# Two pads of 32 bytes that shift every SBUF tile of a two-block transformer kernel

## The chip, the cores and the metric

The kernel runs on one core of one Trainium2 chip, as one program with one launch. Its metric is the device time in microseconds (us).

## The reference, cut to what matters

Two blocks work on 512 tokens of width 1024, in float32, one after the other. The first block has two layers and carries 256 context tokens through its first layer as well, so its matrices have 768 columns there and 512 in the second layer. Each layer is a modulated norm, a projection `px = h @ w_in + b_in`, three mixers (a bidirectional chunked mLSTM, a gated spatial unit, an axial convolution), an output projection and a feed-forward part:

```
x = x + g1 * (y_x @ w_out[l])
x = x + g2 * swiglu(rmsnorm(x) * (1 + sc2) + sh2, w_gu[l], w_down[l])    # 1024 -> 2 x 2816 -> 1024
```

The second block has a dilated windowed attention in three groups (`a_w_in` of 80 x 128 columns), then a sliding-window attention with sinks, and after each a layer norm and a gate:

```
x = layer_norm(ALPHA * x + mixer(x)); x = x + sigmoid(x @ ple_w_gate[i]) * (p[i] @ ple_w_proj[i])
```

Nearly all arithmetic is in these dense products.

## The kernel before, in words

Every activation lies feature-major: 128 features on the partitions, eight such tiles of 1024 features, tokens along the free axis. A dense product is cut into output tiles of 128 features. The weights of one such tile, eight blocks of 128 x 128, come by one DMA into one of four buffers `raw0` to `raw3` (SP's queue, `load`).

Float32 accuracy is made out of three one-pass products in the type `fp32r`. GpSimd (POOL) splits the weights in `split_weights`: `w_hi` is the rounded upper part (line 442), `w_lo = raw - w_hi` the rest (line 444), and `w_lo` is written over `raw`. It does so in two halves for each output tile, one tile ahead of TensorE. For some tiles of the second block ScalarE makes the upper part and POOL only the rest (`split_lower`, line 457). The activations are split too: `XH` and `XL` (normed input of a product), `HH` and `HL` (the feed-forward part's inner values), `XH2`/`XL2` and `YH2`/`YL2` (second block; `YH` and `YL` in the trace). `gemm_step` then issues, for each of the eight blocks, hi x H (line 463), hi x L (464) and lo x H (466), with 512 moving columns, and again with 256 where the context tokens are carried. The in-projection of the first block does the same in `three` (lines 1668 to 1670). A small product in the second block has its own weights `PWH`, `PWL` and operands `PH`, `PL` (lines 837 to 839). In every one of these the weights are the stationary operand and are loaded anew for each matmul.

Each engine runs its own list of instructions, and semaphores tie them together: POOL waits for TensorE to be done with the tile before last (`s_tile`), TensorE waits for the split (`s_split`) and for a free pair of PSUM banks (`s_evac`), ScalarE (ACT) empties the banks, VectorE (DVE) does residuals, norms and the lower halves. Nothing in these lists depends on an address.

All SBUF tiles are laid out by `place` (lines 208 to 217). A tile without `addr` goes to the cursor, which then moves on by the tile's size rounded up to 32 bytes; a tile with `addr` overlays another. The cursor starts at the first multiple of 64 past what the compiler holds back, which is byte 16512, or 129 x 128:

```
        raw = [place(f"raw{i}", [P, KT * P]) for i in range(RING)]
        w_hi = [place(f"w_hi{i}", [P, KT, P], FP32R) for i in range(2)]
        w_lo = [place(f"w_lo{i}", [P, KT, P], FP32R, addr=addr_of[f"raw{i}"]) for i in range(RING)]
        ...
        XH = place("XH", [P, KT, T], FP32R)
        XL = place("XL", [P, KT, T], FP32R)
```

Past `XL` come the small tiles and then, from `work` (line 271), the mixers' tiles, over which `HH` and `HL` lie. The second block starts its own layout at the address of `tri` (line 509) for `YH2`, `YL2`, `PWH`, `PWL`, `PH` and `PL`, and lays `X2`, `XH2` and `XL2` over `XH` and `XL`. Following the sizes gives the bytes past a multiple of 128 at which each operand starts; inside an operand every block is a multiple of 512 bytes further on, so a block's start has the same remainder.

| operand | address before | past a multiple of 128 |
|---|---|---|
| raw, w_lo, w_hi | 16512 to 36992 | 0 |
| Z, X | 41088, 57600 | 0 |
| ones | 57024 | 64 |
| XH, XL; XH2, XL2 | 82176, 106752; 98560, 114944 | 0 |
| HH, HL | 149184, 173760 | 64 |
| YH2, YL2 | 143808, 160192 | 64 |
| PWH, PWL; PH, PL | 198080, 189888; 208320, 212416 | 64 |
| YC, AC | 210720, 216864 | 32 |

Of the kernel before, what the change touches and what calls it, by code (L numbers as in the profile page):

```python
# [20 lines left out]
P = 128  # L21
# [181 lines left out]
def build_program(nc, xT, cT, cb_d, pc_d, fin_d, srow_d, consts_d, sguw_d, wg_d, wmod_d, win_d, wout_d, wgu_d, wdn_d,  # L203
# [4 lines left out]
    def place(name, shape, dt=FP32, addr=None):  # L208
        size = 4
        for s in shape[1:]:  # L210
            size *= s
        if addr is None:
            addr = cursor[0]
            cursor[0] += size + (-size) % 32
        assert addr + size <= nc.sbuf_usable_end, (name, addr + size, nc.sbuf_usable_end)
        addr_of[name] = addr
        return nc.alloc_sbuf_tensor_at(name, shape, dt, offset=addr)

    stack = ExitStack()
    with stack:  # L220
        def sem(name):
            return stack.enter_context(nc.semaphore(name))


        raw = [place(f"raw{i}", [P, KT * P]) for i in range(RING)]
        w_hi = [place(f"w_hi{i}", [P, KT, P], FP32R) for i in range(2)]
        w_lo = [place(f"w_lo{i}", [P, KT, P], FP32R, addr=addr_of[f"raw{i}"]) for i in range(RING)]
# [7 lines left out]
        XH = place("XH", [P, KT, T], FP32R)  # L235
        XL = place("XL", [P, KT, T], FP32R)

        tri = place("tri", [P, 2, P])
        mskd = place("mskd", [P, 2, P])
        mskr = place("mskr", [P, 2, P], FP32R, addr=addr_of["mskd"])  # L240
# [2786 lines left out]
```

## Time and profile before

| | |
|---|---|
| three runs | 2586.6 us median (2584.41 to 2588.71) |
| profiled execution, first to last instruction | 2586.4 us |
| TensorE (PE) busy | 2522.5 us, 98% of the span, 14594 matmuls |
| PE weight loads (PEld) busy | 2083.7 us, 81% |
| POOL busy | 1544.1 us, 60% |
| DVE busy | 1386.4 us, 54% |
| ACT busy | 776.3 us, 30% |
| DMA | 99 GB/s on average |

The profile is of one execution; its span lies 0.2 us from the median of the runs. Matmuls overlap in the pipeline, so the duration shown for one (some 400 ns) is longer than the distance between the starts of two that follow each other; that distance is called the pitch here, and it is read from the starts in the timeline. Busy shares are averages over stages.

### The profile page before, as it was taken

What the parts mean: (1) busy time and instruction counts of PE and PEld (TensorE: products, weight loads), DVE (VectorE), ACT (ScalarE), POOL (GpSimd) and SP (SyncE); (2) the same over time, 40 slices, a digit from 0 to 9 for tenths busy, and PEclk for the clock granted to TensorE, in tenths of its full rate; (3) what the DMA queues carried; (4) which work ended last, traced back from release to release, by engine and by line L of the source; (5) the groups of instructions that cost most, each with busy time, mean ns of one, the idle gap of its engine ahead of it and who ended that gap; (6) DMA issues with size and microseconds to landing.
All of it is one profiled execution on the core that took longest, in us unless ns stands there. A gap on an engine that the chain in (4) does not pass through costs nothing.

```text
span 2586.4 us, 39643 instructions
## 1 busy us (share of the span) xinstructions
PE 2522.5 (98%) x14594; PEld 2083.7 (81%) x14594; DVE 1386.4 (54%) x2065; ACT 776.3 (30%) x1620; POOL 1544.1 (60%) x1625
## 2 busy tenths in 40 slices
PE   6999999999999999999999999999999999999999
PEld 4888988888888886888788887778888888777876
DVE  5864556742853758726433333444444545556754
ACT  3224353111111123244321212222222222443544
POOL 3433245765766665543777777776666676556563
PEclk9999999999999999999999999999999999999999
DMA  7341142332333322121233232433333333323231
GB/s 280 107 155 41 34 179 86 127 130 65 122 130 98 119 60 69 58 66 42 83 96 94 93 98 82 130 106 100 91 103 96 93 103 94 98 73 98 83 106 65
DMA packets 79264, 255.57 MB, mean 99 GB/s; under 512 B 9872, under 2 KB 13712, under 8 KB 78864
## 3 DMA queue, kind: packets, MB, share of 16 engines
q1 hardware_dynamic: 63136, 213.21, 25.8%
q10 hardware_dynamic: 15984, 40.40, 5.1%
q8 instruction: 94, 1.54, 0.3%
q14 instruction: 50, 0.41, 0.1%
HBM read 236.28 MB, written 2.10 MB: 92 GB/s over the span
## 4 chain that ended last, share of the span: by engine, by line
PE 88%; DVE 4%; issue 3%; POOL 2%; ACT 2%; DMA 1%; SPq 0%; ACTq 0%; POOLq 0%; DVEq 0%
PE PS L463 21%; PE PS L466 21%; PE PS L464 21%; PE PS L1668 4%; PE PS L1670 4%; PE PS L1669 4%; PE PS L725 1%; POOL w_lo L444 1%; PE PS L714 1%; PE PS L708 1%; DMA raw<-in_wout 1%; PE PS L1524 1%; POOL w_hi L442 1%; DVE Z L2425 1%; DVE XL L2432 1%
## 5 line engine op out<-in xcount | busy, mean ns | idle before, releaser
L444 POOL TENSOR_TENSOR w_lo<-raw,w_hi 128x512 fp32r<-128x512 f32 (+1 forms) x606 | 880.5, 1453 | 50.6
L463 PE MATMUL PS<-XH,w_hi 128*128 128x512 f32 (+1 forms) x2080 | 782.7, 376 | 16.5 <-DVE XL L2432 3.3
L464 PE MATMUL PS<-XL,w_hi 128*128 128x512 f32 (+1 forms) x2080 | 755.6, 372 | 0.0
L466 PE MATMUL PS<-XH,w_lo 128*128 128x512 f32 (+1 forms) x2080 | 707.2, 373 | 0.0
L437 POOL TENSOR_TENSOR word<-ones 128x1 f32<-128x1 f32 x303 | 93.7, 309 | 869.4 <-PE PS L466 544.2
L463 PEld LDWEIGHTS PS<-XH,w_hi 128*128 128x128 f32 x2080 | 392.2, 189 | 118.6 <-issue 9.3
L442 POOL TENSOR_SCALAR w_hi<-raw 128x512 fp32r<-128x512 f32 (+1 forms) x606 | 482.0, 795 | 0.0
L464 PEld LDWEIGHTS PS<-XL,w_hi 128*128 128x128 f32 x2080 | 392.4, 189 | 70.0
L466 PEld LDWEIGHTS PS<-XH,w_lo 128*128 128x128 f32 x2080 | 362.5, 188 | 55.1
L1668 PE MATMUL PS<-XH,w_hi 128*128 128x512 f32 (+1 forms) x640 | 230.9, 361 | 8.4 <-DVE XL L2432 8.4
L1670 PE MATMUL PS<-XH,w_lo 128*128 128x512 f32 (+1 forms) x640 | 224.9, 351 | 0.0
L1669 PE MATMUL PS<-XL,w_hi 128*128 128x512 f32 (+1 forms) x640 | 224.8, 351 | 0.0
L2530 DVE TENSOR_TENSOR X<-X,Z 128x768 f32 (+3 forms) x60 | 86.0, 1433 | 228.6 <-ACT Z L2051 216.9
L463 PE MATMUL PS<-HH,w_hi 128*128 128x512 f32 (+1 forms) x528 | 187.6, 355 | 3.6 <-DVE HL L2896 3.6
L464 PE MATMUL PS<-HL,w_hi 128*128 128x512 f32 (+1 forms) x528 | 179.4, 354 | 0.0
L2494 DVE CUSTOM_DVE_ANT_0 cprod<-modv,cb 128x1024 f32<-128x1024 f32 x96 | 164.2, 1710 | 18.0 <-DMA modv<-in_wmod 15.1
L2891 DVE SCALAR_TENSOR_TENSOR Z<-TH,Z 128x768 f32<-128x768 f32 (+1 forms) x44 | 50.0, 1136 | 207.5 <-ACT Z L2032 206.4
L466 PE MATMUL PS<-HH,w_lo 128*128 128x512 f32 (+1 forms) x528 | 158.8, 355 | 0.0
L457 POOL TENSOR_TENSOR w_lo<-raw,w_hi 128x512 fp32r<-128x512 f32 x56 | 83.6, 1512 | 106.3 <-ACT w_hi L1051 84.9
L951 ACT ACTIVATE Z<-PS 128x512 f32<-128x512 f32 x99 | 58.7, 594 | 292.3 <-PE PS L466 279.5
L1668 PEld LDWEIGHTS PS<-XH,w_hi 128*128 128x128 f32 x640 | 121.5, 190 | 27.5 <-issue 9.6
L1670 PEld LDWEIGHTS PS<-XH,w_lo 128*128 128x128 f32 x640 | 121.3, 190 | 17.3
(346 smaller groups left out, 3507.0 us busy)
## 6 DMA issues: line engine op xcount, KB each, us to landing
raw<-in_wgu SPq DMA_DIRECT2D x88, 512.0 KB, 3.5
raw<-in_wa SPq DMA_DIRECT2D x80, 512.0 KB, 3.5
modt<-in_wmod SPq DMA_DIRECT2D x48, 512.0 KB, 9.9
raw<-in_win SPq DMA_DIRECT2D x48, 512.0 KB, 3.5
modv<-in_wmod ACTq DMA_DIRECT2D x48, 512.0 KB, 4.7
raw<-in_wdn SPq DMA_DIRECT2D x32, 512.0 KB, 3.6
QS<-Z ACTq DMA_DIRECT2D x96, 128.0 KB, 2.6
raw<-in_wout SPq DMA_DIRECT2D x16, 512.0 KB, 3.5
```

The costliest lines, as they stand in the source:

```text
L437: pool.tensor_tensor(word[:, 0:1], ones[:, 0:1], ones[:, 0:1], ALU.mult)
L442: pool.tensor_scalar(hi, src, 1.0, 0.0, ALU.mult, ALU.add).then_inc(s_hi, 1)
L444: pool.tensor_tensor(lo, src, hi.bitcast(FP32), ALU.subtract).then_inc(s_split, 1)
L457: pool.tensor_tensor(w_lo[s % RING][:, ks, :], src, w_hi[s % 2][:, ks, :].bitcast(FP32), ALU.subtract).then_inc(s_split, 1)
L463: pe.matmul(acc(s)[:, a:b], hi, rh[:, i, a:b], start=i == 0, stop=False)
L464: pe.matmul(acc(s)[:, a:b], hi, rl[:, i, a:b], start=False, stop=False)
L466: last = pe.matmul(acc(s)[:, a:b], lo, rh[:, i, a:b], start=False, stop=i == k - 1)
L1668: pe.matmul(out, hi, XH[:, i, a:b], start=first, stop=False)
L1669: pe.matmul(out, hi, XL[:, i, a:b], start=False, stop=False)
L1670: return pe.matmul(out, lo, XH[:, i, a:b], start=False, stop=i == KT - 1)
L2494: last = dve.tensor_tensor_reduce(out=cprod[:], in0=modv[slots + u][:], in1=cb[:, n, :], scale=0.5, scalar=0.0, op0=ALU.mult, op1=ALU.add, ...
L2530: dve.tensor_tensor(x, x, Z[:, s % 4, 0:w], ALU.add).then_inc(s_used, 1)
```

## The change

Two tiles of eight floats, 32 bytes, that nobody uses are placed: `lead` ahead of `raw0` and `lead2` ahead of `tri`. No instruction is added, removed or moved.

```diff
+        place("lead", [P, 8])
         raw = [place(f"raw{i}", [P, KT * P]) for i in range(RING)]
...
         XL = place("XL", [P, KT, T], FP32R)
 
+        place("lead2", [P, 8])
         tri = place("tri", [P, 2, P])
```

All from `raw0` to `XL` moves up by 32 bytes, all from `tri` on by 64. The weights, Z, X, XH, XL, XH2 and XL2 then start 32 bytes past a multiple of 128, HH, HL, YH2, YL2, PWH, PWL, PH and PL at a multiple of 128, YC and AC at 96 past one. The distance from the weights to XH and XL stays what it was; that to HH, HL, YH2 and YL2 grows by 32.

## Rows read from the trace of the kernel before

**Rows 1.** The page's head and engines, and its row of TensorE's granted clock
```profile
span 2586.4 us, 39643 instructions
PE 2522.5 (98%) x14594; PEld 2083.7 (81%) x14594; DVE 1386.4 (54%) x2065; ACT 776.3 (30%) x1620; POOL 1544.1 (60%) x1625
...
PEclk9999999999999999999999999999999999999999
```

**Rows 2.** The chain that ended last, by engine, and one of its pieces
```profile
PE 88%; DVE 4%; issue 3%; POOL 2%; ACT 2%; DMA 1%; SPq 0%; ACTq 0%; POOLq 0%; DVEq 0%
...
10.85 13.55 DMA modt<-in_wmod
```

**Rows 3.** PE's groups by form: names, shapes, count | busy us, mean ns | idle
```profile
L463 PE MATMUL PS<-XH,w_hi 128*128 128x512 f32 x1664 | 665.3, 400 | 16.5 <-DVE XL L2432 3.3 <-ACT TH L2353 2.6 <-DVE XL L1310 2.2
...
L1668 PE MATMUL PS<-XH,w_hi 128*128 128x512 f32 x384 | 156.8, 408 | 8.4 <-DVE XL L2432 8.4
...
L463 PE MATMUL PS<-HH,w_hi 128*128 128x512 f32 x352 | 138.0, 392 | 3.6 <-DVE HL L2896 3.6
...
L463 PE MATMUL PS<-XH,w_hi 128*128 128x256 f32 x416 | 117.4, 282 | 0.0
...
L463 PE MATMUL PS<-YH,w_hi 128*128 128x512 f32 x216 | 86.8, 402 | 0.8 <-POOL w_lo L457 0.8
...
L1668 PE MATMUL PS<-XH,w_hi 128*128 128x256 f32 x256 | 74.2, 290 | 0.0
...
L463 PE MATMUL PS<-HH,w_hi 128*128 128x256 f32 x176 | 49.7, 282 | 0.0
```

**Rows 4.** PE's timeline: start us, length us; first and last of 384 matmuls on XH, XL
```profile
1403.04 0.39 PE L463 MATMUL PS<-XH,w_hi 128*128 128x512 f32 x1
...
1492.03 0.40 PE L466 MATMUL PS<-XH,w_lo 128*128 128x512 f32 x1
```

**Rows 5.** PE's timeline: first and last of 162 matmuls on HH, HL
```profile
1500.22 0.39 PE L463 MATMUL PS<-HH,w_hi 128*128 128x512 f32 x1
...
1537.08 0.39 PE L466 MATMUL PS<-HH,w_lo 128*128 128x512 f32 x1
```

**Rows 6.** PE's timeline, 768 tokens: where HH, then XH, then HH again begins
```profile
551.76 0.40 PE L463 MATMUL PS<-HH,w_hi 128*128 128x512 f32 x1
...
618.34 0.39 PE L463 MATMUL PS<-XH,w_hi 128*128 128x512 f32 x1
...
752.61 0.39 PE L463 MATMUL PS<-HH,w_hi 128*128 128x512 f32 x1
```

**Rows 7.** PE's timeline: first and last of twelve matmuls on PH, PL
```profile
2253.45 0.39 PE L837 MATMUL PS<-PH,PWH 128*128 128x512 f32 x1
...
2255.94 0.39 PE L839 MATMUL PS<-PH,PWL 128*128 128x512 f32 x1
```

**Rows 8.** PE's groups by form: plain float32 matmuls against `ones`
```profile
L849 PE MATMUL PS<-Z,ones 128*128 128x512 f32 x32 | 14.3, 599 | 1.4 <-ACT Z L1091 1.4
...
L1663 PE MATMUL PS<-AC,ones 128*128 128x512 f32 x8 | 3.9, 592 | 0.0
```

**Rows 9.** Groups by form of DVE and ACT: tiles 32 past and others
```profile
L2731 DVE TENSOR_TENSOR AC<-AC,MU 128x512 f32<-128x512 f32 x2 | 1.3, 688 | 23.9 <-ACT MU L2201 23.9
L2891 DVE SCALAR_TENSOR_TENSOR Z<-TH,Z 128x512 f32<-128x512 f32 x22 | 15.3, 693 | 143.4 <-ACT Z L2032 143.4
...
L2278 ACT ACTIVATE YC<-AC 128x1024 f32<-128x1024 f32 x1 | 1.1, 1062 | 0.0
L2057 ACT ACTIVATE SQ<-X 128x512 f32<-128x512 f32 x14 | 8.9, 632 | 11.4 <-DVE X L2530 11.4
```

**Rows 10.** Groups of POOL, with its idle time and what ended it
```profile
L444 POOL TENSOR_TENSOR w_lo<-raw,w_hi 128x512 fp32r<-128x512 f32 (+1 forms) x606 | 880.5, 1453 | 50.6
L442 POOL TENSOR_SCALAR w_hi<-raw 128x512 fp32r<-128x512 f32 (+1 forms) x606 | 482.0, 795 | 0.0
L437 POOL TENSOR_TENSOR word<-ones 128x1 f32<-128x1 f32 x303 | 93.7, 309 | 869.4 <-PE PS L466 544.2 <-PE PS L1670 300.4 <-DMA raw<-in_win 16.3
```

**Rows 11.** Busy us and count by engine (PE, PEld, DVE, ACT, POOL), clock, DMA share, GB/s
```profile
1404.00:1491.00 87.00, 87.00 (x376) 70.54 (x375) 28.59 (x22) 17.41 (x31) 68.39 (x79) 1.00 0.31 97
```

## The prediction

> **What bounds the kernel now.** I read the engines' shares first, then the chain, then PE's groups and starts. PE is busy in 2522.5 of 2586.4 us, at its higher clock level of 2.4 GHz (granted 0.9 or more in every slice) [rows 1], and 88% of the chain is PE [rows 2]. In a stretch of dense product all 87.00 us of 87.00 are PE, POOL needs 68.39 of them, DVE 28.59, ACT 17.41 [rows 11]. So within the products the end is set by the pitch of the matmuls, and a nanosecond there is a nanosecond of the kernel, as often as there are matmuls. Counting each hi x H row three times (hi x L and lo x H have the same counts), there are on XH and XL (1664 + 384) x 3 = 6144 matmuls of 512 columns and (416 + 256) x 3 = 2016 of 256; on HH, HL, YH2, YL2 (352 + 216) x 3 = 1704 of 512 and 176 x 3 = 528 of 256 [rows 3].
>
> The change touches only addresses, so what decides is whether the pitch depends on them, and the trace of before says that it does. On XH and XL, weights and operand both 0 past a multiple of 128, 383 steps take 1492.03 - 1403.04 = 88.99 us: 232.4 ns [rows 4]. On HH and HL, with the weights still at 0 and the operand at 64, 161 steps take 36.86 us: 228.9 ns [rows 5]. Same lines of code, columns, weight buffers and layer, a few us apart. On PH and PL, with both weights and operand at 64, eleven steps take 2.49 us: 226.4 ns, with starts shown to 0.01 us, so 225 to 227 [rows 7]; I use 226.5. 512 columns alone are 213.3 ns at 2.4 GHz, so each family pays something on top: 19.1, 15.6 and 13.2 ns. Where 768 tokens are carried, a 512 and a 256 together take 134.27 / 384 = 349.7 ns on XH and 66.58 / 192 = 346.8 ns on HH [rows 6]: there too HH is 2.9 ns cheaper.
>
> The Trainium skill ("SBUF — State Buffer", Who interferes with whom, and Specifications) says that PE has two read ports of its own, one for the moving operand and one for weights, that PE never waits on anyone, and that SBUF is made of 16-byte lines. By that rule a shift by 32 bytes, two whole lines, does nothing. The rows contradict its strict form: two operands that differ in placement alone differ by 3.5 ns in pitch. The rule's outcome for this change is the first rival below.
>
> **The change part by part.**
>
> 1. *XH, XL, XH2, XL2 with their weights, from (0, 0) to (32, 32)* (weights, operand, past 128). No row has an fp32r matmul at 32, so this is bounded. One end is (0, 0) as it is, 232.4 ns. The end below is (64, 64), 226.5 ns, the only row in which weights and operand were shifted together, as here. 32 lies halfway between the two, so I take the middle, 229.5 ns, which is also next to HH's 228.9. That is -2.9 ns x 6144 = -17.8 us for the 512s. For the 256s I take half of it, as a 256 reads half the bytes: -1.45 x 2016 = -2.9 us. Ends: at (64, 64)'s value -5.9 x 6144 - 2.95 x 2016 = -42.2 us; nothing is a gain of 0; a loss is the second rival.
>
> 2. *HH, HL, YH2, YL2 from (0, 64) to (32, 0).* The operand goes to where XH was, the weights leave it. Bounds from the rows: 228.9 to 232.4 ns, 0 to +3.5 each; and 226.5 below, -2.4. I take +1.7 x 1704 = +2.9 us and +0.85 x 528 = +0.4 us. Ends: -2.4 x 1704 - 1.2 x 528 = -4.7 us, and +3.5 x 1704 + 1.75 x 528 = +6.9 us.
>
> 3. *PWH, PWL, PH, PL from (64, 64) to (0, 0):* 96 matmuls by at most 5.9 ns, +0.6 us; the gates' fp32r matmuls on XH are as few again and I leave them at 0, within half a us.
>
> 4. *Plain float32 matmuls* (sums against `ones`, transposes): AC, which lies 32 past, takes 592 ns where Z at 0 takes 599 [rows 8]. No penalty at 32; nothing, within their 20 us a tenth of a per cent of the kernel at most.
>
> 5. *DVE, ACT, POOL.* On DVE a 128x512 with AC at 32 takes 688 ns, one on Z and TH at 0 takes 693; on ACT 1024 columns at 32 take 1062 ns, less than twice the 632 of 512 columns at 0 [rows 9]. So nothing. POOL's split has no row at 32. Its cover is large: POOL idles 869.4 us ahead of 303 tiles, nearly all of it for PE, 2.87 us a tile [rows 10]. Either split may grow by half, 0.4 or 0.7 us a half tile, before all of it is late: 2 x (0.40 + 0.73) = 2.26 us. A faster PE takes 24 x 2.9 ns = 0.07 us from that slack. Hidden; where it ran out, POOL would set the pace.
>
> 6. *DMAs into raw, X and modt* land 32 past. Only the opening is bound by them: the chain has 13.55 us of the modulation's weights [rows 2]. At zero to a tenth of it, 0 to +1.4 us; I take 0, since raw arrives ahead of POOL almost everywhere (16.3 us of 869.4 behind a DMA, [rows 10]).
>
> Sum: -17.8 - 2.9 + 2.9 + 0.4 + 0.6 = -16.8 us. All of it falls inside dense products where PE alone sets the pace, so I let it through whole. The profiled span of 2586.4 becomes 2569.6; the median of the runs is 0.2 us higher, so 2569.8, rounded 2570 us. With everything else as above and part 1 between -10 and -30 us, this case spans 2560 to 2580.
>
> **The rivals.**
>
> *Only the distance between weights and operand counts, or nothing does.* XH is 49280 bytes from w_hi before and after, PH is 10240 from PWH, HH 116288 from w_hi. Past a multiple of 256 these are 128, 0 and 64, and the pitches are 232.4, 226.5 and 228.9: in order of that distance, which explains the rows as well as the absolute address does. Then part 1 is 0, PH stays, and HH and YH2 go from 64 to 96 past 256, halfway to XH's: +1.7 x 1704 + 0.85 x 528 = +3.3 us, 2590 us; 2584 to 2592 with the ends. By the rule of the Trainium skill cited above the time would be 2587 us. For it: the order. Against it: it needs a period of 256 that only three placements show.
>
> *Slower: a start 32 past costs a further piece.* Suppose that operands are fetched in pieces of 64 bytes, 16 columns. All fp32r operands in the rows start on such a boundary; 2048 bytes that start 32 past one touch 33 pieces and not 32, and 1024 bytes 17 and not 16. If the extra piece is paid, at 16 columns / 2.4 GHz = 6.7 ns, it is 6.7 x (6144 + 2016) = +54.7 us, with part 2 +58 us: 2645 us; if the piece is hidden in half of them, 2617. For it: the spread of the pitches between families, 5.9 ns, is about one such piece. Against it: AC at 32 pays none, though in plain float32, where the columns pass more slowly [rows 8]. It decides from the point where the pitch on XH lies over 232.9 ns, as 0.6 ns on 8160 matmuls is the 5 us that can be told from no change.
>
> *Faster by all that placement costs.* If 32 is as good as (64, 64) and HH no worse than now: -42 and -2, 2542 us. For it: nothing sets 32 apart from 64 but the rows' silence. Against it: the middle is nearer to the rows.
>
> **How the numbers follow.** The forecast of part 1 to 6: 0.33. Faster by nearly all: 0.18. Only the distance, or nothing: 0.22. The further piece: 0.27. A difference of 0.2%, 5 us, is about what can be told from no change. The first two give faster 0.51, the third mostly same, 0.21 with small overlaps, the fourth slower, 0.28. The range goes from 2536, just below the third case's 2542, to 2618, where half of the further piece is paid; the upper half of that rival and a little below are left out, some 0.18.
>
> **What would show it.** Starts on XH and XL between 1403 and 1492 us: a pitch of 228 to 231 ns is the forecast; 232.4 is the first rival, 237 to 239 the second, under 228 the third. On HH and HL 229 to 232. The counts, the order and POOL's 1453 and 795 ns should stay; if POOL, DVE or DMA groups change by more than their own spread, part 5 or 6 was wrong. The forecast is wrong if XH's pitch stays or rises.

## The result, and the profile after

The changed kernel takes 2592.57 us (median of 7 runs, 2591.42 to 2594.06), the kernel before 2585.69 us (7 runs): a ratio of 1.0026, 95% interval 1.0016 to 1.0035. It is slower by 6.9 us, a little more than the 0.2% that can be told from no change. I had forecast 2570 us.

The page's head and engines after the change, which answer to [rows 1]:

```profile
span 2590.1 us, 39643 instructions
...
PE 2527.2 (98%) x14594; PEld 2080.5 (80%) x14594; DVE 1392.0 (54%) x2065; ACT 776.6 (30%) x1620; POOL 1544.0 (60%) x1625
```

The profiled execution of the changed kernel took 2592.48 us, 2.4 more than its span. By the same difference the span of 2586.4 us before belongs to an execution of some 2588.7 us, the upper end of its runs, and not, as I had it, to one 0.2 us from the median. So the two spans differ by 3.7 us only, and the medians by 6.9. Both traces have the same 14594 matmuls in the same order, so their steps can be matched one by one: those over 270 ns (over 140 with 256 columns), which hold the waits, take 3.3 us less in the trace after, and all others some 7 us more.

The same stretches of PE's timeline as before (start us, length us), two lines further down in the code. First the 384 matmuls on XH and XL, which answer to [rows 4], then 160 on HH and HL, which answer to [rows 5]:

```profile
1402.43 0.39 PE L465 MATMUL PS<-XH,w_hi 128*128 128x512 f32 x1
...
1491.43 0.39 PE L468 MATMUL PS<-XH,w_lo 128*128 128x512 f32 x1
...
1500.09 0.39 PE L468 MATMUL PS<-HH,w_lo 128*128 128x512 f32 x1
...
1537.19 0.39 PE L468 MATMUL PS<-HH,w_lo 128*128 128x512 f32 x1
```

XH: 89.00 us in 383 steps, 232.4 ns as before. HH: 37.10 us in 159 steps, 233.3 ns, where it had 228.9. So the operand that went from 0 to 32 past 128 together with its weights shows nothing, and the one whose distance to the weights grew by 32 lost 4.4 ns on each matmul. With 768 tokens, where HH, XH and HH again begin, which answers to [rows 6]:

```profile
550.85 0.39 PE L465 MATMUL PS<-HH,w_hi 128*128 128x512 f32 x1
...
618.27 0.39 PE L465 MATMUL PS<-XH,w_hi 128*128 128x512 f32 x1
...
752.53 0.39 PE L465 MATMUL PS<-HH,w_hi 128*128 128x512 f32 x1
```

A 512 and a 256 together take 67.42 / 192 = 351.1 ns on HH (346.8 before) and 134.26 / 384 = 349.6 on XH (349.7 before). Over all starts less than 270 ns apart, YH2's mean pitch went from 229.2 to 233.4 and HH's at 512 tokens from 229.0 to 233.4. That makes 528 x 4.3 ns (HH, 768 tokens, pairs) + 528 x 4.4 (HH, 512) + 648 x 4.2 (YH2) = 2.3 + 2.3 + 2.7 = 7.3 us, against the 6.9 measured. All steps on XH and XL under the limits above together changed by 0.5 us, and downwards, so the loss lies on HH and YH2. POOL's groups stayed as they were, beside [rows 10], and so did the shares in the stretch of dense product, beside [rows 11]:

```profile
L446 POOL TENSOR_TENSOR w_lo<-raw,w_hi 128x512 fp32r<-128x512 f32 (+1 forms) x606 | 878.8, 1450 | 50.6
L444 POOL TENSOR_SCALAR w_hi<-raw 128x512 fp32r<-128x512 f32 (+1 forms) x606 | 481.8, 795 | 0.0
L439 POOL TENSOR_TENSOR word<-ones 128x1 f32<-128x1 f32 x303 | 95.3, 314 | 873.2 <-PE PS L468 545.9 <-PE PS L1672 301.6 <-DMA raw<-in_win 17.5
```
```profile
1404.00:1491.00 87.00, 87.00 (x376) 70.52 (x376) 28.24 (x22) 17.30 (x30) 67.91 (x78) 1.00 0.30 96
```

### The profile page after: what moved, and what is told of

The parts are those of the page before. It is cut to its first block, busy times and chain, and to the rows that moved or that the text cites. A ratio compares the mean times of both kernels' runs of the same rounds, so it can differ in the third digit from the quotient of the medians.

```text
span 2590.1 us, 39643 instructions
## 1 busy us (share of the span) xinstructions
PE 2527.2 (98%) x14594; PEld 2080.5 (80%) x14594; DVE 1392.0 (54%) x2065; ACT 776.6 (30%) x1620; POOL 1544.0 (60%) x1625
## 4 chain that ended last, share of the span: by engine, by line
PE 88%; DVE 4%; issue 3%; POOL 2%; ACT 2%; DMA 1%; SPq 0%; ACTq 0%; POOLq 0%; DVEq 0%
PE PS L465 21%; PE PS L468 21%; PE PS L466 21%; PE PS L1670 4%; PE PS L1672 4%; PE PS L1671 4%; PE PS L727 1%; POOL w_lo L446 1%; PE PS L716 1%; PE PS L710 1%; PE PS L1526 1%; DMA raw<-in_wout 1%; POOL w_hi L444 1%; DVE Z L2427 1%; DVE XL L2434 1%
## 5 line engine op out<-in xcount | busy, mean ns | idle before, releaser
L446 POOL TENSOR_TENSOR w_lo<-raw,w_hi 128x512 fp32r<-128x512 f32 (+1 forms) x606 | 878.8, 1450 | 50.6
L2532 DVE TENSOR_TENSOR X<-X,Z 128x768 f32 (+3 forms) x60 | 85.3, 1422 | 233.4 <-ACT Z L2053 221.2
```

The source lines that it names most:

```text
L446: pool.tensor_tensor(lo, src, hi.bitcast(FP32), ALU.subtract).then_inc(s_split, 1)
L2532: dve.tensor_tensor(x, x, Z[:, s % 4, 0:w], ALU.add).then_inc(s_used, 1)
```

## The experiments

My forecast rested on the address of the operand and its weights by itself, the first rival on the distance between the two. The experiments move one or the other. "Distance" below is the operand's address minus that of w_hi, past a multiple of 256: before, 128 for XH and XL and 64 for HH, HL, YH2 and YL2; after, 128 and 96. Only under "Which weights" does w_lo have another distance than w_hi. Pitches are read from the first and last of the 384 matmuls on XH near 1400 to 1490 us, as in [rows 4], and of the HH stretch behind it.

**The first pad alone.**

```diff
+        place("lead", [P, 8])
         raw = [place(f"raw{i}", [P, KT * P]) for i in range(RING)]
```

> Only the pad ahead of raw: everything moves by 32 together, weights, XH and XL to 32 past 128, HH, HL, YH2, YL2 to 96 past; every distance from the weights stays that of before. Distance theory (the pitch hangs on the distance from the weights to the operand, taken past a multiple of 256): HH 228.9 ns and XH 232.4 as before, 2586 us, ratio 1.000. Address theory (the pitch hangs on where the operand itself starts: 64 past 128 is good, 0 and 32 are bad): HH at 96 is neither, 229 to 232.4, ratio 1.000 to 1.003. Weights theory (weights at 32 spoil HH's pitch): HH 232, YH 233, ratio 1.0026 as in the changed kernel.

2586.59 us against 2586.10, ratio 1.0001 (0.9992 to 1.0010). HH, now at 96 past 128 with its weights at 32, from PE's timeline (154 matmuls):

```profile
1500.09 0.39 PE L467 MATMUL PS<-HH,w_lo 128*128 128x512 f32 x1
...
1535.11 0.39 PE L467 MATMUL PS<-HH,w_lo 128*128 128x512 f32 x1
```

35.02 / 153 = 228.9 ns, as before; XH 232.4. Everything moved, and the pitches stayed. The weights at 32 are not the cause, and an address that is no multiple of 64 costs nothing by itself here.

**The second pad alone.**

```diff
+        place("lead2", [P, 8])
         tri = place("tri", [P, 2, P])
```

> Only a pad of 32 ahead of tri: weights, XH and XL stay at 0, HH, HL, YH2 and YL2 go to 96 past 128, 96 from the weights past 256, which is their distance in the changed kernel. Distance theory: HH 232 and YH 233 ns as in the changed kernel, 2592 us, ratio 1.0026. Weights theory: HH stays at 228.9, ratio 1.000. Address theory: HH at 96, neither 64 nor 0, 229 to 232.4, ratio 1.000 to 1.003, and the same HH pitch as with only the first pad.

2593.97 us, ratio 1.0029 (1.0018 to 1.0041): the whole loss. HH is at 96 past 128 as in the run above, but its distance is 96 (157 matmuls):

```profile
1500.10 0.39 PE L467 MATMUL PS<-HH,w_lo 128*128 128x512 f32 x1
...
1536.50 0.39 PE L467 MATMUL PS<-HH,w_lo 128*128 128x512 f32 x1
```

36.40 / 156 = 233.3 ns. The same operand address, 149216, gives 228.9 with the weights 32 higher and 233.3 here. This pair refutes the address theory and carries the distance theory.

**Distance 0 for all.** To see whether the theory also gains:

```diff
+        place("mid", [P, 32])
         X = place("X", [P, KT, T])
...
+        place("lead2", [P, 16])
         tri = place("tri", [P, 2, P])
```

> A pad of 128 ahead of X and one of 64 ahead of tri: XH, XL, HH, HL, YH2 and YL2 all start at 0 past 128, as XH does before, but at a distance of 0 past 256 from the weights (128 for XH before), as PH has from PWH. Distance theory: all of them at PH's 226.5 ns; 5.9 x 6144 + 2.9 x 2016 + 2.4 x 1704 + 3 x 528 = -48 us, 2538 us, ratio 0.981. Address theory: XH stays at 232.4, HH and YH2 at 0 get it too, +6 us, 2592 us, ratio 1.0025.

2566.20 us, ratio 0.9922 (0.9908 to 0.9935). XH, still at 0 past 128:

```profile
1399.01 0.39 PE L465 MATMUL PS<-XH,w_hi 128*128 128x512 f32 x1
...
1485.83 0.39 PE L468 MATMUL PS<-XH,w_lo 128*128 128x512 f32 x1
```

86.82 / 383 = 226.7 ns, and HH 226.7 too, which is PH's pitch of [rows 7]. The expected 2538 us were missed mainly because distance 0 brings nothing where 512s and 256s are mixed. In the output projection and the feed-forward part at 768 tokens their order is 512, 512, 256, 256, 512, 256, and a pair there takes 351.0 ns on XH and 351.1 on HH, against 350.7 and 346.8 before (means over all such steps, where [rows 6] takes the first and last of one stretch). The gain is nearly all in the 512-token part: 4319 matmuls on XH from a mean of 232.5 to 227.5 ns, 21.6 us; HH at 768 tokens gives back 528 x 4.3 ns = 2.3 us. It is the mixing that matters and not the 768 tokens: in the in-projection of the same layer, where 24 matmuls of 512 columns run before 24 of 256, the 512s fall from a mean of 232.5 to 228.6 ns.

**The other distances.** Five more kernels place the operands with pads ahead of X and of tri alone, as in the diff above: 64 and none, 192 and none, 96 and none, 160 and none, 32 and 96.

> A pad of 64 ahead of X: XH and XL start at 64 past 128 and at a distance of 192 past 256; HH, HL, YH2 and YL2 at 0 past 128 and at a distance of 128 past 256, which is XH's before. Distance theory: HH and YH2 at 232.4 ns; XH at whatever 192 gives, which no row shows: 228.9 if 192 is as 64 (a gain of 24 us, 2570 us with HH's loss of 7 taken off), 226.5 to 234 in all. Address theory: XH at 64 gets 228.9, HH at 0 gets 232.4, 2570 us.

> A pad of 192 ahead of X: XH and XL go to a distance of 64 past 256 from the weights (HH's before), HH, HL, YH2 and YL2 to 0. Distance theory, with the pitches measured so far for each distance: XH at 512 tokens from 232.5 to 229.0 ns, 4319 x -3.5 = -15 us; a 512 and a 256 together at 768 tokens from 350.9 to 346.8, 1824 x -4.1 = -7 us; HH and YH2 at 512 tokens 226.8 to 228, -2 us; HH at 768 tokens 351, +2 us: 2564 us, ratio 0.9915. Address theory: XH at 64 past 128 gets 228.9 here too, but HH at 0 gets 232: 2570 us.

> A pad of 96 ahead of X: XH at a distance of 224, HH and YH2 at 160 past 256. Distance theory: some pitch between 226.7 and 233.5 for each, the same one that another tile shows at the same distance; if only 0 and 64 are good, both lie at 232 to 233.5 and the time is 2590 us. A theory in which the distance counts from either side (224 as 32) would have XH between 226.7 and 229, 2570 us.

> A pad of 160 ahead of X: XH at a distance of 32, HH and YH2 at 224 past 256. Distance theory: XH between the 226.7 ns of 0 and the 229.0 of 64, so about 228, 4319 x -4.5 = -19 us, 2567 us with a loss or gain of HH of some 3 us; HH as XH in the kernel with a pad of 96. If only multiples of 64 count as good, XH stays at 232 to 233 and the time is 2590 us.

> A pad of 32 ahead of X and one of 96 ahead of tri: XH at a distance of 160, HH and YH2 at 192 past 256. Distance theory: HH and YH2 at 192 show XH's 233.3 ns of the kernel with a pad of 64, and XH at 160 what HH shows with a pad of 96; some 2590 us. Address theory: HH at 64 past 128 (as before) keeps 228.9.

Their times, one run each but for the second: 2591.07 us; 2568.54 us, ratio 0.9932 (0.9916 to 0.9949); 2595.46; 2595.65; 2599.34; before 2586.10 for the first and 2586.88 for the others. First and last of the 384 matmuls on XH, for distance 192:

```profile
1399.64 0.39 PE L464 MATMUL PS<-XH,w_hi 128*128 128x512 f32 x1
...
1489.00 0.39 PE L467 MATMUL PS<-XH,w_lo 128*128 128x512 f32 x1
```

for distance 64:

```profile
1393.08 0.40 PE L464 MATMUL PS<-XH,w_hi 128*128 128x512 f32 x1
...
1480.76 0.39 PE L467 MATMUL PS<-XH,w_lo 128*128 128x512 f32 x1
```

for distance 32:

```profile
1404.25 0.40 PE L464 MATMUL PS<-XH,w_hi 128*128 128x512 f32 x1
...
1493.61 0.39 PE L467 MATMUL PS<-XH,w_lo 128*128 128x512 f32 x1
```

and for distance 160:

```profile
1405.12 0.39 PE L465 MATMUL PS<-XH,w_hi 128*128 128x512 f32 x1
...
1494.85 0.40 PE L468 MATMUL PS<-XH,w_lo 128*128 128x512 f32 x1
```

Divided by 383 they give 233.3, 228.9, 233.3 and 234.3 ns. In the first two of these kernels XH starts at 64 past 128 alike; by the address theory both would show 228.9. All kernels together, those of the next three parts left out, at 512 tokens in such stretches, and at 768 tokens as the mean of a 512 plus that of a 256 (starts over 270 and 140 ns apart left out):

| distance | XH, 512 tokens, ns | HH, 512 tokens, ns | a pair on XH | a pair on HH |
|---|---|---|---|---|
| 0 | 226.7 | 226.7 | 351.0 | 351.0 to 351.1 |
| 32 | 233.3 | | 350.0 | |
| 64 | 228.9 | 228.9 | 346.9 | 346.8 |
| 96 | | 233.3 | | 351.1 |
| 128 | 232.4 or 233.3 | 233.3 | 349.7 to 350.7 | 353.3 |
| 160 | 234.3 | 234.3 | 349.0 | 349.0 |
| 192 | 233.3 | 233.3 | 348.9 | 348.9 |
| 224 | 233.3 | 233.3 | 350.7 | 350.7 |

The columns for 512 tokens agree although XH and HH lie elsewhere, in different kernels. At 128 more than one repeating pattern of starts shows (232.4 is one of seven matmuls, 233.3 one of two), even in one kernel: before, XH has 232.4 ns near 1450 us and XH2, at the same distance, 233.3 from 2482 to 2515 us. So the distance alone does not fix the pitch to the last nanosecond. At 512 tokens two distances of eight are good; in the pairs 64 is the best, and 0 is among the worst. That 32 lies between 0 and 64 in pitch, which I had expected, is refuted: 233.3. So is a distance that counts from either side: 64 and 192 would then be equal, and they differ by 4.4 ns (228.9 and 233.3).

**Which weights.**

```diff
+        place("apart", [P, 32])
         w_hi = [place(f"w_hi{i}", [P, KT, P], FP32R) for i in range(2)]
```

> A pad of 128 between raw (with w_lo in it) and w_hi: XH stays at 128 past 256 from w_hi and goes to 0 from w_lo, HH and YH2 stay at 64 from w_hi and go to 192 from w_lo. Two matmuls of three have w_hi as weights. If each matmul pays for the distance of the weights that go with it or are loaded beside it: XH at 512 tokens (2 x 232.5 + 227) / 3 = 230.7 ns, HH (2 x 229 + 233.3) / 3 = 230.4, 2578 us. If only w_hi counts: 232.5 and 229.0, 2586 us. If the worse of the two sets the pitch of all: 232.5 and 233.3, 2592 us.

2591.94 us in one run, before 2586.00. XH, at 128 from w_hi and 0 from w_lo:

```profile
1402.16 0.40 PE L464 MATMUL PS<-XH,w_hi 128*128 128x512 f32 x1
...
1491.52 0.40 PE L467 MATMUL PS<-XH,w_lo 128*128 128x512 f32 x1
```

233.3 ns, a pitch that distance 128 alone shows too; a third of the weights at the good distance gives nothing, as if the worse ruled. HH, at 64 and 192, shows 228.9 in the stretch near 1515 us and 233.3 in those near 1380 and 1625 us, a mean of 231.9 over all at 512 tokens. Both weights count, but by no simple mean, and what chooses between the two pitches is open.

**Weights or their neighbours.** In all kernels so far Z had moved with the weights. The pad of 128 goes ahead of Z:

```diff
+        place("mid", [P, 32])
         Z = place("Z", [P, 4, T])
...
+        place("lead2", [P, 16])
         tri = place("tri", [P, 2, P])
```

> As the kernel with pads of 128 and 64, but the 128 stand ahead of Z and not of X: XH, XL, HH, HL, YH2 and YL2 are at 0 past 256 from the weights as there, while Z, TH, ident and ones, which lay with the weights in every kernel so far, keep their old distance to XH. If the distance to the weights is what counts: XH and HH at 512 tokens 226.7 ns, 2566 us. If the distance to Z or to the constants counted: XH 232.4 and HH 233, 2590 us.

2569.56 us in one run, and XH:

```profile
1399.34 0.39 PE L465 MATMUL PS<-XH,w_hi 128*128 128x512 f32 x1
...
1486.16 0.39 PE L468 MATMUL PS<-XH,w_lo 128*128 128x512 f32 x1
```

226.7 ns, and HH 226.8. The partner is the weights.

**A version that beats both.** Each operand at its best distance:

```diff
+        TH = place("TH", [P, N_SROW])
+        word = place("word", [P, 8])
+        eps_c = place("eps_c", [P, 2])
         raw = [place(f"raw{i}", [P, KT * P]) for i in range(RING)]
...
-        TH = place("TH", [P, N_SROW])
...
-        word = place("word", [P, 8])
-        eps_c = place("eps_c", [P, 2])
+        place("mid", [P, 16])       # ahead of X
...
+        place("lead2", [P, 16])     # ahead of tri
...
+        place("lead3", [P, 48])     # ahead of YH2
...
-        X2 = place("X2", [P, KT, SEQ], addr=addr_of["XH"])
+        X2 = place("X2", [P, KT, SEQ], addr=addr_of["XH"] - 64)     # XH2, XL2, QK likewise
```

> Each operand at the best distance that the runs have shown, by moves of addresses alone: TH, word and eps_c ahead of raw, pads of 64 ahead of X and of tri, 192 ahead of YH2, and X2, XH2, XL2 and QK 64 lower. XH, XL, HH and HL are then at 64 past 256 from the weights (a 512 and a 256 together 346.8 ns), XH2, XL2, YH2 and YL2 at 0 (227 ns). Distance theory: against the kernel with a pad of 192, 2495 x -2.0 = -5 us on XH2, 528 x -4.2 = -2 us on HH at 768 tokens, +1 us on HH at 512: ratio to before 0.991, 2562 us. If the moved weights matter by themselves, XH at 768 tokens keeps some 350 and XH2 232, 2585 us.

2563.45 us, ratio 0.9911 (0.9894 to 0.9927), as expected: 0.9% faster than before by addresses alone. From the kernel with distance 0 for all (0.9908 to 0.9935) the times don't tell it apart. XH at 512 tokens:

```profile
1392.22 0.39 PE L465 MATMUL PS<-XH,w_hi 128*128 128x512 f32 x1
...
1479.88 0.39 PE L468 MATMUL PS<-XH,w_lo 128*128 128x512 f32 x1
```

228.9 ns, and 227.0 on XH2 over 119 steps from 1645.15 us on.

## Why the prediction was wrong

- *That the pitch of the matmuls sets the time, and that it hangs on placement*, was right: the loss is pitch times count, 7.3 us worked out and 6.9 measured.
- *Part 1, XH with its weights from (0, 0) to (32, 32), -17.8 and -2.9 us*, is the step that failed. I took the middle between (0, 0) and (64, 64) on the ground that there too weights and operand had moved together. They had not: XH is 128 past 256 from its weights, PH is 0, as I worked out myself under the first rival. Measured: 232.4 ns before and after, 0 us for the 512s and the 256s alike within 0.6 us, and a pitch of XH that stays is what I had named as the sign of being wrong. The 226.5 ns itself stood on one group of twelve matmuls; over all 86 steps under 270 ns on PH and PL the mean is 229.7, and only the later kernels with distance 0 show it in long stretches. The three placements of the trace fitted two readings equally well, and I took one of them with no row that told them apart.
- *Part 2, HH and YH2, +3.3 us*: right in sign, half the size, and by luck, since it rested on the operand's address. Halfway between two known pitches was no estimate: at a distance of 96 the pitch, 233.3 to 233.4 ns, is higher than at 64 and at 128 in the rows (228.9 and 232.4), so it passed the upper end of my bounds: +7.3 us, where the end was +6.9.
- *Part 3*, +0.6 us, rested on the same error as part 1: PH keeps its distance of 0, and the mean of its steps is 229.7 ns before and 230.0 after. *Parts 4 to 6*, nothing on plain float32, DVE, ACT, POOL and the DMAs, held: the groups of [rows 8] take 599 and 592 ns as before, POOL's split 1450 and 795 (1453 and 795), and with the first pad alone, which moves all of them by 32, the ratio is 1.0001. The 20 us of part 4 were too few, without consequence: the matmuls against `ones` are busy for some 50 us, those with `ident` for some 97.
- *The rival of the distance*, at 0.22, is what happened. Its 2590 us are too low because its price for HH and YH2 is that of part 2, and its ends, 2584 to 2592, are not those of part 2, which give 2582 to 2593. Its other half, that no placement counts at all, 2587 us, is refuted by the ratio. *The further piece at 32* is refuted by the first pad: XH at 32 keeps 232.4 ns. *Faster by all that placement costs* needed XH's pitch to fall, and it stayed.
- The Trainium skill ("TensorE: Matmul & The Clock Gate", Step-by-step: what each phase is for) says that the load of the next weights takes no SBUF bandwidth from the running matmul, as each has a read port of its own. The runs do not measure that bandwidth, but they show that the two are not independent, and here the measurement decides: the distance between their addresses moves the pitch from 226.7 to 234.3 ns.

What stays open is the mechanism behind the distance. That the weight load beside a streaming matmul reads the same part of SBUF at the same time is only argued; the runs show that the two addresses matter through their difference and that the neighbours don't. Whether it is the running matmul's own weights that count or those loaded beside it is not separated, since the weights have one remainder in every kernel but one. Why 0 helps where 512s follow each other and not where 256s are mixed in is not shown either.

## What to carry to other kernels

When a trace shows two families of equal instructions with different pitches, list for each operand pair the address and the difference, and count how many readings the rows leave before one is chosen: two pads, one of which moves both and one only one of them, settle it in one run each. Where a price between two known points is wanted, interpolate only over a quantity that is known to act smoothly; an address remainder is not one. In this kernel, which is bound by fp32r matmuls with fresh weights, the operand's address minus that of the weights, past a multiple of 256, was worth 0.9% for a few hundred bytes of pads; whether the same distances are the good ones in another kernel is not shown, but its pitches would tell.

## What the runs showed of the hardware that was not expected

With fresh weights for each matmul, fp32r matmuls of 512 columns follow each other at 226.7 ns at the best distance (0 past 256) and 233.3 to 234.3 at the worst, at a granted clock of 1.00; between 226.7 and 233.3 lie 16 columns at 2.4 GHz, 6.7 ns. The pitches between them are means over a fixed pattern: at distance 128, seven matmuls with starts 228 to 241 ns apart that repeat, at distance 64 three with 226, 229 and 232. A period of 128 bytes is ruled out (0 and 128 differ by 5.7 ns); all that was measured fits one of 256, and a longer one of 512 is not needed: distances of 64 and of 320 past 512, in the last kernel and in that with a pad of 192, both give 228.9 ns on XH.
